# One exponential per head and direction pair in the SSD scores of a hybrid encoder trunk

## The reference, cut to what matters

```python
def step(state, inp):                      # one chunk of 128 tokens; a group has 8 heads
    acum = jnp.cumsum(dtc * a, axis=1)
    diff = acum[:, :, None] - acum[:, None, :]
    decay = jnp.exp(jnp.where(causal, diff, -jnp.inf))
    cb = jnp.einsum('blgn,bsgn->blsg', cc, bc)
    scores = cb[..., None] * decay * dtc[:, None]
    y = jnp.einsum('blsge,bsgep->blgep', scores, xc)
    y = y + jnp.einsum('blgn,bgepn->blgep', cc, state) * jnp.exp(acum)[..., None]
    ...
y = y_fwd + y_bwd + xs * d_skip
y = y * silu(z)                            # then a group RMSNorm
```

## Time and profile before

| | us |
|---|---|
| median of 3 runs | 1332.7 |
| profiled execution | 1333.24 |
| its span, first to last instruction | 1331.4 |
| TensorE busy | 1316.7 (99%) |
| VectorE, ScalarE, GpSimd busy | 770.4, 642.1, 624.0 |
| mean granted TensorE clock | 0.996 of full |

### The profile page before, as it was taken

How to read it: one execution, slowest core, us unless ns; L and a number is a source line. 1 busy time by engine, 2 the same in 40 slices (tenths; PEclk the granted TensorE clock), 3 DMA queues, 4 the chain that set the end, 5 groups by cost and what they waited for, 6 DMA issues and landing times.

```text
span 1331.4 us, 16274 instructions
## 1 busy us (share of the span) xinstructions
PE 1316.7 (99%) x6540; PEld 1112.0 (84%) x6540; DVE 770.4 (58%) x842; ACT 642.1 (48%) x1029; POOL 624.0 (47%) x294
## 2 busy tenths in 40 slices
PE   9999999999999999999999999999999999999997
PEld 7878878888898888888889988888998888888887
DVE  5857486840079998885000863436379988882002
ACT  6654777652355544444223586555555444443221
POOL 3344461245524654445553354755535644445551
PEclk9999999999999999999999999999999999999998
DMA  5342111123223333333332323311223333333331
GB/s 207 96 119 80 53 35 41 64 80 96 83 92 95 95 99 102 100 92 87 103 90 89 124 64 95 95 60 65 83 96 97 101 102 97 95 89 96 93 87 64
DMA packets 41147, 119.77 MB, mean 90 GB/s; under 512 B 4592, under 2 KB 11632, under 8 KB 41072
## 3 DMA queue, kind: packets, MB, share of 16 engines
q1 hardware_dynamic: 39712, 116.43, 28.5%
q10 hardware_dynamic: 1360, 2.29, 0.6%
HBM read 116.35 MB, written 2.23 MB: 89 GB/s over the span
## 4 chain that ended last, share of the span: by engine, by line
PE 92%; DVE 5%; ACT 1%; SPq 1%; DMA 0%; issue 0%; ACTq 0%; DVEq 0%
PE bank L345 26%; PE bank L349 26%; PE bank L348 26%; DVE sqacc L674 1%; PE bank L1819 1%; PE bank L1817 1%; PE bank L1818 1%; PE bank L2057 1%; PE bank L1370 1%; PE bank L1550 1%; PE bank L1553 1%; PE bank L398 1%; PE bank L2039 1%; PE bank L1337 1%; PE bank L1580 1%; PE bank L1339 1%
## 5 line engine op out<-in xcount | busy, mean ns | idle before, releaser
L318 POOL TENSOR_TENSOR wlo<-raw,whi 128x1024 fp32r<-128x1024 f32 (+2 forms) x214 | 530.9, 2494 | 621.5 <-ACT whi L312 621.4
L345 PE MATMUL bank<-xw_hi,whi 128*128 128x512 f32 (+1 forms) x1272 | 474.9, 374 | 1.6 <-DVE xw_lo L734 0.9
L349 PE MATMUL bank<-xw_hi,wlo 128*128 128x512 f32 (+1 forms) x1256 | 466.8, 372 | 0.0
L348 PE MATMUL bank<-xw_lo,whi 128*128 128x512 f32 (+1 forms) x1256 | 466.7, 372 | 0.0
L312 ACT ACTIVATE whi<-raw 128x1024 fp32r<-128x1024 f32 (+2 forms) x215 | 219.7, 1025 | 206.0 <-DMA raw<-in_fout 112.6
L345 PEld LDWEIGHTS bank<-xw_hi,whi 128*128 128x128 f32 x1272 | 239.7, 188 | 44.2 <-issue 2.1
L349 PEld LDWEIGHTS bank<-xw_hi,wlo 128*128 128x128 f32 x1256 | 236.5, 188 | 41.6
L348 PEld LDWEIGHTS bank<-xw_lo,whi 128*128 128x128 f32 x1256 | 236.7, 188 | 40.2 <-issue 0.2
L607 DVE RECIPROCAL small<-small 128x2 f32<-128x2 f32 x8 | 1.3, 164 | 315.2 <-ACT small L532 313.9
L760 DVE SCALAR_TENSOR_TENSOR cbuf<-ubuf,par,cbuf 128x510 f32<-128x510 f32 x100 | 168.8, 1688 | 3.5
L345 PE MATMUL bank<-g_hi,whi 128*128 128x512 f32 (+1 forms) x396 | 145.3, 367 | 0.2
(11 more groups left out here) (282 smaller groups left out, 1458.8 us busy)
## 6 DMA issues: line engine op xcount, KB each, us to landing
raw<-in_fin SPq DMA_DIRECT2D x88, 512.0 KB, 3.6
raw<-in_fout SPq DMA_DIRECT2D x32, 448.0 KB, 3.3
raw<-in_gin SPq DMA_DIRECT2D x25, 512.0 KB, 3.6
raw<-in_hin SPq DMA_DIRECT2D x22, 512.0 KB, 3.7
raw<-in_hout SPq DMA_DIRECT2D x16, 512.0 KB, 3.7
raw<-in_fout SPq DMA_DIRECT2D x16, 512.0 KB, 3.5
raw<-in_gout SPq DMA_DIRECT2D x8, 512.0 KB, 3.7
xres<-in_x SPq DMA_DIRECT2D x8, 256.0 KB, 4.6
```

The lines of the kernel that those rows point to most:

```text
L318: engine.tensor_tensor(wlo[s][:, 0:n], raw[s][:, 0:n], whi[s][:, 0:n].bitcast(F32), ALU.subtract).then_inc(w_lo, 1)
L345: first = nc.tensor.matmul(out_ap, wh, ah, start=start, stop=False)
L348: nc.tensor.matmul(out_ap, wh, al, start=False, stop=False)
L349: return first, nc.tensor.matmul(out_ap, wl, ah, start=False, stop=stop)
```

## The change: what it does

The exponent of a head and direction is formed whole by one matmul over 32 rows. Its stationary operand `steady` holds picks of the head (16 rows) and the rows of token s (`u`, high and low part by block, 8 rows); its moving operand `moving` holds the decays of token l (16 rows) and block indicators. Both are filled by DMA through DRAM (`decays`). There is no -2^30 any more: a predicated copy on VectorE takes the backward exponent where the source token is later (`con("later")`), and one exponential of 512 columns a head follows. The diagonal of the backward direction is no longer in the sum; it goes into an own term: the input times (D + dt times the column sum of B*C), computed as 32 rows (`dve_own_rows`), spread to 64 partitions a head by DMA (`sp_own`) and multiplied on GpSimd (`pool_own`). VectorE adds it with `whole`. `pool_far` goes to ScalarE (`act_late_x`).

Shortened diff (declarations, layout and constants are left out):

```diff
 # pe_hin: after block 18; dve_hin: after blocks 19, 21, 22; pool_hin: with block 17
+                if j == 18:
+                    pe_own_sums(pe)
...
+                if j == 19:
+                    dve_own_rows(dve)
                 if j == 21:
-                    dve_both_ways(dve, 0)
+                    dve_either_way(dve, 0)
                 if j == 22:
-                    dve_both_ways(dve, 1)
+                    dve_either_way(dve, 1)
...
+                if at == BASE["hin"] + TURN0:
+                    pool_b_times_c(pool)
 # act_hin: act_decay_tables(act) early in place of act_picks and of the DMA to at_both; dve_dt: two steps more
+        def act_decay_tables(act):            # 128x1024 and 128x512, ACT.Copy of broadcast constants
...
+        def sp_decays_out(sp):                # before load(hin+10)
+            sp.wait_ge(sem("dt_dve"), 14)
+            for i in range(4):
+                sp.dma_start(decays[i], rows_of[i][:].bitcast(F32)).then_inc(sem("rows_out"), 16)
+        def sp_decays_in(sp, q):              # before load(hin+11+q): four DMAs each, q = 0..3
...
+        def pool_b_times_c(pool):
+            pool.wait_ge(sem("hin_silu"), 12)
+            for g in range(2):
+                nc.gpsimd.tensor_tensor(ebuf[2 + g][:], ck(xbc, 8 + g), ck(xbc, 10 + g), ALU.mult)
+        def pe_own_sums(pe):
+            for g in range(2):
+                last = nc.tensor.matmul(bank[(2, 7)[g]][0:64, :], ones[:, 0:64], ebuf[2 + g][:], start=True, stop=True)
+        def dve_own_rows(dve):                # three scalar_tensor_tensor of 32x512
+        def sp_own(sp, c):
+            if c == 0:
+                sp.wait_ge(sem("own_rows"), 3)
+                sp.dma_start(own_rows, sqbuf[0][32:64, :]).then_inc(sem("rows_out"), 16)
+                sp.wait_ge(sem("rows_out"), 96)
+                sp.wait_ge(mm, BASE["mla"])
+            for u in range(2):
+                row = 2 * c + u
+                sp.dma_start(ck(m_ffn, c)[u * HDIM:(u + 1) * HDIM, :],
+                             own_rows[row:row + 1, :].broadcast_to([HDIM, T])).then_inc(sem(f"chunk_in{c}"), 16)
+        def pool_own(pool, c):
+            pool.wait_ge(sem(f"chunk_in{c}"), 16 + 32)
+            nc.gpsimd.tensor_tensor(ck(xbc, c), ck(xbc, c), ck(m_ffn, c), ALU.mult).then_inc(sem("own_part"), 1)
+        def act_late_x(act, i):
+            for h in range(GHEADS):           # 128x64 each, scale by a column of cols
+                last = nc.scalar.activation(wx[1][:, at], xtok[1][:, at], ACT.Copy, scale=cols[:, weight:weight + 1])
 # pool_ssd
             for n in range(3, HEADS):
                 pool_mask(pool, n)
-                if n < 3 + NBLK:
-                    pool_far(pool, n - 3)
+                if n < 3 + KD:
+                    pool_own(pool, n - 3)
 # VectorE
-            dve.wait_ge(sem("ssd_exp"), EXPS * (n + 1))
-            nc.vector.tensor_tensor(ebuf[n % 4][:], ebuf[n % 4][:], abank(n, 1)[:], ALU.add)
+            dve.wait_ge(sem("a_mm"), 2 * n + 2)
+            nc.vector.copy_predicated(fore, mask, back).then_inc(sem("ssd_way"), 1)
...
+            def whole(c):
+                dve.wait_ge(sem("ssd_y"), 2 * c + 1)
+                dve.wait_ge(sem("own_part"), c + 1)
+                nc.vector.tensor_tensor(reach[c % 2][:], reach[c % 2][:], ck(xbc, c), ALU.add)
             for n in range(HEADS):
                 c = n // 2
                 if n % 2:
                     far_part(c)
-                elif n:
+                if n + 2 < HEADS:
+                    dve_either_way(dve, n + 2)
+                if n and n % 2 == 0:
                     near_part(c - 1)
-                if n + 2 < HEADS:
-                    dve_both_ways(dve, n + 2)
-                if n % 2:
-                    skip(c)
-                elif n:
+                    whole(c - 1)
                     gated(c - 1)
 # act_exps
-            (four exponentials of abank(n, 0) with bias, four of abank(n, 1))
+            act.wait_ge(sem("ssd_way"), n + 1)
+            if n >= 4:
+                act.wait_ge(sem("y_mm"), n - 3)
+            nc.scalar.activation(ebuf[n % 4][:], abank(n, 0)[:], ACT.Exp).then_inc(sem("ssd_exp"), 1)
 # act_ssd
                 act_exps(act, n)
+                if n < 3 + NBLK:
+                    act_late_x(act, n - 3)
 # pe_spread
-                pe.wait_ge(sem("ssd_both"), n - 1)
+                pe.wait_ge(sem("ssd_exp"), n - 1)
             for d in range(2):
-                (never_r by eye_r, then pick by at_both: two matmuls over 128 rows)
+                rows = slice(32 * (2 * (n // GHEADS) + d), 32 * (2 * (n // GHEADS) + d + 1))
+                nc.tensor.matmul(abank(n, d)[:], steady[rows, j * P:(j + 1) * P], moving[rows, :], start=True, stop=True)
 # sp: reach(c) waits for ssd_y 2c-2 (gated(c-2)) where it waited for ssd_far c-1
```

More of the change, by code:

```diff
@@ L1002, in build_program @@
         group_rstd = [rstd, sqacc]
-        dt_f, dta_f, sum_f, a_f = (wx[0][0:64, i * T:(i + 1) * T] for i in range(4))
+        dta_f, sum_f, a_f = (wx[0][0:64, i * T:(i + 1) * T] for i in range(3))
         u_f, w_f = (sqbuf[i][0:64, :] for i in range(2))
@@ L1028, in build_program @@
         gt_rows = nc.dram_tensor("gt_rows", (64, T), F32).ap()
+        OWN_AT = next(f for f in range(TOTAL) if AFTER[f] >= BASE["mla"] - 1)
         REACH_AT = next(f for f in range(TOTAL) if AFTER[f] >= BASE["mla"])
@@ new lines, in pe_own_sums @@
+        def pe_own_sums(pe):
+            pe.wait_ge(sem("b_times_c"), 2)
+            pe.wait_ge(sem("dt_dve"), 15)
+            for g in range(2):
+                last = nc.tensor.matmul(bank[(2, 7)[g]][0:64, :], ones[:, 0:64], ebuf[2 + g][:], start=True, stop=True)
+            last.then_inc(sem("own_sums"), 1)
+        own_rows = nc.dram_tensor("own_rows", (32, T), F32).ap()
+        def dve_own_rows(dve):
+            dve.wait_ge(sem("own_sums"), 1)
+            parts = [sqbuf[g][32:64, :] for g in range(2)]
+            for g in range(2):
+                nc.vector.scalar_tensor_tensor(out=parts[g], in0=bank[(2, 7)[g]][32:64, :],
+                                               scalar=con("ofgroup", 2)[32:64, g:g + 1], in1=dt_f[32:64, :],
+                                               op0=ALU.mult, op1=ALU.mult).then_inc(sem("own_rows"), 1)
+            dve.wait_ge(sem("own_rows"), 2)
+            nc.vector.scalar_tensor_tensor(out=parts[0], in0=parts[0], scalar=con("skips", 1)[32:64], in1=parts[1],
+                                           op0=ALU.add, op1=ALU.add).then_inc(sem("own_rows"), 1)
@@ L1204, in abank, with dve_either_way @@
             return bank[2 * (1 - n % 2) + d]
-        def dve_both_ways(dve, n):
-            dve.wait_ge(sem("ssd_exp"), EXPS * (n + 1))
-            nc.vector.tensor_tensor(ebuf[n % 4][:], ebuf[n % 4][:], abank(n, 1)[:], ALU.add).then_inc(
-                sem("ssd_both"), 1)
+        def dve_either_way(dve, n):
+            dve.wait_ge(sem("a_mm"), 2 * n + 2)
+            mask = con("later").bitcast(mybir.dt.uint32).unsqueeze(1).broadcast_to([P, NBLK, P])
+            fore, back = (abank(n, d)[:].rearrange("p (b l) -> p b l", b=NBLK) for d in range(2))
+            nc.vector.copy_predicated(fore, mask, back).then_inc(sem("ssd_way"), 1)
         def dve_ssd(dve):
@@ L1248, in dve_ssd @@
             near_part(KD - 1)
+            whole(KD - 1)
             dve.wait_ge(sem("hin_zsilu"), KD)
@@ L2284, in _ @@
             for f in range(3, TOTAL):
+                if f == BASE["hin"] + 10:
+                    sp_decays_out(sp)
+                if 0 <= f - BASE["hin"] - 11 < 4:
+                    sp_decays_in(sp, f - BASE["hin"] - 11)
                 if f == BASE["hin"] + 16:
@@ L2287, in _ @@
                     sp_reach(sp, 1)
+                if f == OWN_AT:
+                    for c in range(KD):
+                        sp_own(sp, c)
                 if f == REACH_AT:
@@ L2493 @@
     cst, rope, glac = _constants()
+    cst[32:32 + HEADS, CCOLS["skips"]] = np.asarray(inputs["ssd_d"])[0]
     data |= {"cst": cst, "rope": rope, "glac": glac}
```

152 lines of the change are left out of this document (80 added, 72 removed).

## The result

| | before | after |
|---|---|---|
| median, us | 1332.72 (4 runs) | 1342.15 (4 runs, 1339.87 to 1345.59) |
| ratio | | 1.0078, 95% interval 1.0065 to 1.0091 |
| profiled execution, its span | 1333.24, 1331.4 | 1345.59, 1343.7 |
| mean granted TensorE clock | 0.996 | 0.987 |

The change costs 9.4 us by the medians, 10.4 by the ratio. The profiled execution was the slowest of the four, so 3.4 us of what follows belongs to it alone. First the page, the counterpart of the earlier trace rows: GpSimd has 11.8 us more, VectorE 13.2 more, ScalarE 18.7 less.

The account below looks back on a forecast made before the run. GpSimd's queue and port become the bound: from mask 3 at 162.6, 28.2 + 5.8 + 2.0 end mask 13 at 198.6; plus 8.5, `rope(0)` at 207.1, +9.9, so 1342.6 by the median; range 1334 to 1351.

Parts of the forecast that it names:

- GpSimd, 22 instructions: GpSimd's queue, mask 3 to mask 13: 11 masks, 8 own products, 3 sums of squares at 1.28, 28.2 us.
- port, masks 3 to 13: Shared SBUF port: 11 meetings with VectorE's `whole` and `gated`, GpSimd losing 0.53 each, 5.8 us; bounds 0 to 7.6.
- idle before mask 5: Start of the loop: VectorE's order leaves GpSimd idle, 0.9 or 2.6 us by who goes first; 2.0 taken.
- end of mask 13 to `rope(0)`: End of the heads: last copy, exponential, matmuls, far and low parts take 8.5 us, so `rope(0)` starts at 207.1.
- `hin`: a term put at nothing: In `hin`: own sums 1.9, spreads lose 1.4, block 23 0.5 later; added steps and tables hide, uncovered up to 4 us.
- a stall in `hin`: Sign of being wrong: a stall in `hin` before block 23.
- The late exponential 3: Start of the loop: copies behind block evictions delay ScalarE; exponential 3 ends at 162.6, where mask 3 began at 159.71.
- GpSimd and its port: In the heads: GpSimd's queue becomes the bound, 6.4 a pair against TensorE's 4.25, plus port waits; forecast case, 68%.
- TensorE saves and nobody collects: In the heads: each spread loses two matmuls, 0.46 us, a pair 4.25 instead of 5.17, but TensorE waits for GpSimd.
- The clock rival: In the heads: waiting puts TensorE to its lower clock, about 8.3 a pair, 1352 us; chance 12%.
- Behind `rope(0)`: After the heads: the earlier idle and lower-clock cost is paid in much the same way; nothing later differs.
- `reach`: hidden: `reach` refilled after `gated(c-2)`: four DMAs of 2.6 us against two to three heads of time, at most 1 us.

Follow-up runs that it names:

- e3: Changed kernel with the four decay DMAs, and what follows them, one weight load later in SyncE's queue: 1341.82 us, ratio 1.0078.
- e4: Changed kernel with each own product on GpSimd made on 8 of 512 columns, so its output differs: 1339.39 us, ratio 1.0056.
- e5: Changed kernel with each 32-row spread matmul issued three times, four more a head: 1344.3 us, ratio 1.0093.
- e7: Changed kernel with the edits of e1, e2 and e9 together: 1335.52 us, ratio 1.0023.
- e9: Changed kernel with ScalarE's two table copies after the MLA deviation and the decay DMAs moved accordingly: 1340.76 us, ratio 1.0067.
- e2: Changed kernel with the predicated copies of heads 1 and 2 one block earlier in VectorE's queue: 1340.09 us, ratio 1.0061.
- e1: Changed kernel with the running sum of a pair kept in PSUM instead of `reach`: 1335.63 us, ratio 1.0028.
- e6: Kernel before the change, with the running sum kept in PSUM as in e1: 1331.43 us, ratio 0.9993.
- e10: e7 with `reach` refilled after `near` and two refills sent among the own rows: 1330.58 us, ratio 0.9999.
- e12: e10 with own products spread evenly and GpSimd's last sums of squares waiting for VectorE's three low parts: 1329.22 us, ratio 0.9983.

## Why the prediction came out as it did

Forecast 1342.5, measured 1342.15. The mechanism (GpSimd's queue with the port) was right; that the number came within 0.4 us is in part luck, since several terms were off and partly cancelled: `hin` cost 1.8 us more than said, the stretch of the masks 2.4 less, its end 1.1 more.

| step | predicted | measured |
|---|---|---|
| block 23's eviction against before | +0.5 | +3.7, of it 1.4 in the profile's start |
| mask 3 behind that eviction | 6.8 | 6.67 |
| GpSimd, 22 instructions | 28.2 | 22 x 1.23 = 27.1 |
| port, masks 3 to 13 | 11 x 0.53 = 5.8 | 9 x 0.45 = 4.1 |
| idle before mask 5 | 2.0 | 2.46 |
| mask 3 to the end of mask 13 | 36.0 | 33.6 |
| end of mask 13 to `rope(0)` | 8.5 | 9.6 |
| `rope(0)` | 207.1 | 208.96 |

- **`hin`: a term put at nothing.** The first eviction of the program came at 33.58 against 32.18, since TensorE's granted clock was lower before it in this execution (0.83 from 25 to 35, against 1.00 before). That 1.4 is not the change's: e3, e4, e5 and e7 have the change and their first eviction between 31.69 and 31.97. Of the other 2.3, the stall before 73.69 is 1.3; the own sums took 2.0 (said: 1.9) and the spreads gave 1.2 (said: 1.4). The prediction had put tables and steps at nothing, with VectorE and ScalarE at 58% and 48% of the span as cover, and had named a stall in `hin` as a sign of being wrong; this part of it was. The cover was an average over the span, while from 40 to 50 us VectorE was busy for 9.81 of 10 us already in the kernel before. What exactly makes the stall stays open: not the DMAs (e3), hardly the tables (e9), more likely the added steps.
- **The late exponential 3: right**, by time (6.67 against 6.8) and by e2 (2.1 us where 2.4 hung on it in the prediction's sum).
- **GpSimd and its port: right, a little oversized.** One that starts behind its neighbour costs 1.23, since two overlap by 0.04; a meeting costs 0.45, not 0.53, and 9 instructions met one, not 11. The 0.53 misread its row: the mask of the earlier trace rows lost 1.65 less 1.28, that is 0.37; that it began 0.16 behind VectorE's instruction was no loss. VectorE loses more than the prediction said, 0.95 of a `gated` of 1.64; it did not matter for the sum, but it made VectorE the second bound, which e4 found. The Trainium skill, "SBUF — State Buffer", on contention of the two engines, says that a VectorE instruction with at most one SBUF input does not contend; e1's groups agree (692 and 700 ns), and 6.5 us went with it. From its rule of a lock for the whole instruction the prediction had worked out 0.69 a meeting; the rows show that the one engine waits for the other, but that GpSimd loses 0.45.
- **TensorE saves and nobody collects: right, the saving undersized.** The prediction took 0.23 for each 32-row matmul and so 0.46 saved a head. The two of a head run side by side and take 0.43 together, where the four of before took 1.02 to 1.13: 0.6 to 0.7 saved. It changed nothing in the sum, as the prediction said of its bounds; e5 put some 7 us back into the loop and 1.0 showed.
- **Prices**: copy 0.69 (0.7), exponential 0.60 (0.65), eight late inputs 2.00 (2.1).
- **The clock rival** had its fall (0.50 from 165 to 175, 0.66 from 195 to 205) but hardly its price. From 168 to 178 VectorE waits for TensorE nowhere, so nothing of it passes on. Near 196 a `y` takes 1.97 us where 1.09 is its length at full clock, and VectorE waits 1.38 for it (both lines below): 0.9 at most. How much of that is in the 1.1 by which the end came out longer is not separated, since `gated(5)` there also took 1.64 where 0.7 was counted. Its premise, that an idle of 1.97 us puts TensorE to its lower level, does not hold every time: in e6's profile TensorE stood 1.96 us before `rope(0)` and the clock stayed at 1.00. Without the port waits it still fell in e1 (0.83 from 165 to 185); in e10 and e12 it stayed at 1.00 through the heads.
- **Behind `rope(0)`**: the prediction let the lower clock behind the idle time be paid in the same way. It was not: TensorE stood 0.88 us and then ran at full clock. That the rest took as long as before came from a fall near 960 us, in this execution and in e9's and in no other profile.

```profile
195.69 1.97 PE L1448 MATMUL bank<-ebuf,xtok 128*64 128x128 f32 x8 [2.07 <-POOL ebuf L1203]
197.69 0.69 DVE L1312 TENSOR_TENSOR reach<-reach,bank 128x512 f32<-128x512 f32 x1 [1.38 <-PE bank L1448]
```

- **`reach`: hidden, as said**, 0.3 in the changed kernel; but it was the next wait in line, 4.6 us once the rest was mended. The prediction had named its DMA after `gated(c-2)` and not its place behind 17 others in SyncE's queue.

## What to carry over

When the bound engine is relieved by work on two others that share a port, read their mean instruction length beside its length alone: the gap times its count (here 4.3 us on GpSimd, 11.1 on VectorE) is what a PSUM operand takes off each queue. It won 6.5 us here, and a tenth of that where those engines had slack. Mend one wait and read the trace again before adding up the next: three repairs worth 10.5 us together showed 7.3 (by ratio) until a DMA's place in the queue was changed. And repair the old kernel in the same way before saying that the new one is faster.

## What the runs showed of the hardware

- A predicated copy of 128x512 between PSUM banks takes 0.69 us; one of 256 columns, there into SBUF, took 0.44. Half the columns are not half the time.
- Two float32r matmuls over 32 rows each, on different groups of rows and into different PSUM banks, run side by side: 0.43 us for a pair of 512 columns with the change from and to 128 rows around it, and 0.23 to 0.34 for each further pair (e5: six in 0.90).
- A GpSimd product of 8 columns took 0.20 us in three cases and 0.65 in five, against 1.27 for 512 (e4): leaving out 98% of the columns saved between half and five sixths. What decides between the two was not found.
- VectorE's three steps of 64x512 beside GpSimd's 128x1024 remainders took 1.9, 2.78 and 2.88 us, close to the 2.7 of such a remainder; their cause, the port, was read from that and not tested.
- A row spread by DMA over 64 partitions costs SyncE 0.67 us of its queue (16 in 10.66), as much as a weight load of the MLA stage (0.58 for 256 or 384 KB). In e7 `reach(2)` could have been sent when `gated(0)` was done, at 164.3; it was sent from 168.16 and was there at 172.8, so 3.9 of its 8.5 us were the place in the queue.
